# Down projections of the MLPs: a fourth step of seven products in each second half, and residual banks added by DMA

## The reference, cut to what matters

```python
h = rms_norm(x, norm_mlp_g[l])
x = x + jnp.square(jax.nn.relu(h @ w_mlp_up[l])) @ w_mlp_down[l]      # 2048 -> 8192 -> 2048
```

## Time and profile before

| | us |
|---|---|
| median of 3 timed runs | 2652.4 (2650.54 to 2652.66) |
| the profiled execution | 2650.98 |
| its span, first to last instruction | 2649.3 |
| TensorE matmul busy in it | 2640.2 |
| VectorE busy | 1986.9 |
| ScalarE busy | 1366.9 |

### The profile page before, as it was taken

How to read it: one execution, slowest core, us unless ns; L and a number is a source line. 1 busy time by engine, 2 the same in 40 slices (tenths; PEclk the granted TensorE clock), 3 DMA queues, 4 the chain that set the end, 5 groups by cost and what they waited for, 6 DMA issues and landing times.

```text
span 2649.3 us, 39598 instructions
## 1 busy us (share of the span) xinstructions
PE 2640.2 (100%) x13478; PEld 2233.5 (84%) x13478; DVE 1986.9 (75%) x2876; ACT 1366.9 (52%) x1865; POOL 30.3 (1%) x64
## 2 busy tenths in 40 slices
PE   9999999999999999999999999999999999999999
PEld 7888888888888888888888888888788888888887
DVE  6687876555555778798797567878787978879886
ACT  6455555444444554555554454456555555455453
POOL 0100000000000000000000000000000000000000
PEclk9999999999999999999999999999999999999999
DMA  7655556665655566556566555545555655655565
GB/s 277 236 175 182 190 173 197 204 201 194 203 191 188 177 199 205 187 196 198 190 206 210 190 176 175 173 150 191 171 175 190 199 198 192 205 190 196 187 205 175
DMA packets 141721, 511.06 MB, mean 193 GB/s; under 512 B 16134, under 2 KB 16439, under 8 KB 141464
## 3 DMA queue, kind: packets, MB, share of 16 engines
q1 hardware_dynamic: 136312, 493.86, 55.9%
q0 software_dynamic: 3840, 12.86, 1.5%
q10 hardware_dynamic: 1440, 2.62, 0.3%
HBM read 505.08 MB, written 4.21 MB: 192 GB/s over the span
## 4 chain that ended last, share of the span: by engine, by line
PE 96%; DVE 2%; ACT 1%; DMA 0%; issue 0%; SPq 0%; ACTq 0%; DVEq 0%
PE acc L1955 26%; PE acc L1952 13%; PE acc L1973 5%; PE acc L1991 4%; PE acc L1993 4%; PE acc L1992 4%; PE pS L1991 3%; PE pS L1993 3%; PE pT L1993 3%; PE pT L1991 3%; PE pS L1992 3%; PE pT L1992 3%; PE acc L1970 2%; PE pO L1991 2%; PE pO L1993 2%; PE pG L1993 2%
## 5 line engine op out<-in xcount | busy, mean ns | idle before, releaser
L1104 DVE TENSOR_TENSOR wlo<-raw,whi 128x1024 fp32r<-128x1024 f32 x938 | 1143.4, 1223 | 446.4 <-ACT whi L614 440.5
L614 ACT ACTIVATE whi<-raw 128x1024 fp32r<-128x1024 f32 x938 | 990.0, 1057 | 793.7 <-PE pT L1993 243.1
L1955 PE MATMUL acc<-a_w,whi 128*128 128x512 f32 x2944 | 935.8, 397 | 0.1
L1952 PEld LDWEIGHTS acc<-a_w,wlo 128*128 128x128 f32 x2944 | 553.2, 188 | 129.4
L1952 PE MATMUL acc<-a_w,wlo 128*128 128x256 f32 x2944 | 578.6, 278 | 0.0
L1955 PEld LDWEIGHTS acc<-a_w,whi 128*128 128x128 f32 x2944 | 451.5, 189 | 2.5 <-DVE a_w L1157 0.8
L1973 PE MATMUL acc<-a_w,whi 128*128 128x512 f32 x592 | 198.4, 404 | 0.0
L825 ACT ACTIVATE t<-acc 128x256 f32<-128x256 f32 x128 | 48.9, 382 | 170.0 <-PE acc L1955 169.9
L1970 PEld LDWEIGHTS acc<-a_w,wlo 128*128 128x128 f32 x592 | 111.4, 188 | 24.5
L1970 PE MATMUL acc<-a_w,wlo 128*128 128x256 f32 x592 | 116.8, 279 | 0.0
L1500 DVE TENSOR_TENSOR t<-acc,t 128x256 f32<-128x256 f32 x128 | 54.0, 422 | 74.9 <-ACT t L825 74.8
(11 more groups left out here) (496 smaller groups left out, 3962.8 us busy)
## 6 DMA issues: line engine op xcount, KB each, us to landing
raw<-stream SPq DMA_DIRECT2D x938, 512.0 KB, 3.4
gbias<-gateb POOLq DMA_DIRECT2D x12, 256.0 KB, 4.1
X<-x_rows POOLq DMA_DIRECT2D x4, 512.0 KB, 6.8
bias_scratch<-brow POOLq DMA_DIRECT2D x8, 256.0 KB, 5.5
q<-bias_scratch POOLq DMA_DIRECT2D x8, 256.0 KB, 3.8
out<-X ACTq DMA_DIRECT2D x8, 256.0 KB, 5.3
xF<-x SPq DMA_DIRECT2D x6, 256.0 KB, 6.8
bias<-bias_scratch POOLq DMA_DIRECT2D x8, 128.0 KB, 4.1
```

Of the source, the lines that this page charges most:

```text
L614: A(whi[:, slot, :], raw[:, slot, :], ACT.Copy).then_inc(s.hi_done, 1)
L1104: TT(wlo[:, slot, :], raw[:, slot, :], whi[:, slot, :].bitcast(F32), SUB).then_inc(s.lo_done, 1)
L1952: low = lambda: MM(ps[:, 0:T], wl, wide[:, k0 + k, 0:T], start=False, stop=False, skip_group_check=True)
L1955: last = MM(ps, wh, wide[:, k0 + k, :], start=start and k == 0, stop=not start and k == KC - 1, skip_group_check=True)
```

## The change

`BLOCK_STEPS` becomes 0 to 3 in both halves, and both halves have one order: 4, 0, 1, 5, 2, 6, 3, 7 (ordinary, seven, seven, ordinary, seven, ordinary, seven, ordinary). In the six groups with two such halves the result banks are no longer added to X by VectorE: ScalarE copies each, scaled, to one of six SBUF buffers (`drain_bank`), and a DMA issued by GpSimd adds the buffer to X (`accum_op`). The part banks of g = 0 are copied by ScalarE; those of g = 1, 2 are added by VectorE at t = 14 and 15 of either half. `WARM` is 8. The GpSimd DMAs' descriptor scratch is set to 4096 bytes.

```diff
-WARM = 5
+WARM = 8
-BLOCK_ORDER = ((4, 0, 5, 1, 6, 2, 7, 3), (3, 4, 0, 5, 1, 2, 6, 7))
-BLOCK_STEPS = ((0, 1, 2, 3), (0, 1, 2))
+NDRAIN = 6
+DRAINS = 8 * 3
+BLOCK_ORDER = ((4, 0, 1, 5, 2, 6, 3, 7), (4, 0, 1, 5, 2, 6, 3, 7))
+BLOCK_STEPS = ((0, 1, 2, 3), (0, 1, 2, 3))
...
+        drain = sb("drain", NDRAIN * COLS)[0].rearrange("p (k c) -> p k c", k=NDRAIN)
...  GpSimd
+            def add(dst):
+                k = added[0]
+                added[0] += 1
+                pool.dma_start(dst, drain[:, k % NDRAIN, :], accum_op=ALU.add).then_inc(drain_added[k % NDRAIN], 16)
+            def add_columns(i, n):
+                for h in range(2):
+                    pool.wait_ge(s.t_evac, 2 * (i + n) + h + 1)
+                    add(X[:, h, COLS * n:COLS * n + COLS])
...  ScalarE
+            def drain_bank(ps, scale, freed):
+                k = drained[0]
+                drained[0] += 1
+                if k >= NDRAIN:
+                    act.wait_ge(drain_added[k % NDRAIN], 16 * (k // NDRAIN))
+                A(drain[:, k % NDRAIN, :], ps, ACT.Copy, scale=scale).then_inc(freed, 1)
+            def drain_parts(layer, g, q):
+                r = phase(layer, g, q)
+                act.wait_ge(s.block_done, BLOCK_CHUNKS_AFTER[r])
...
+                for n in range(4):
+                    A(parts[q][n], (acc[0], acc[1], pV, pN)[n], ACT.Copy).then_inc(s.m_free, 1)
+                    def down_pair(q):
...
+                        for t in range(16):
+                            if t == 14 and not g:
+                                drain_parts(layer, g, q)
+                            if t == 14 and not q:
+                                act.wait_ge(s.rb_ready, 4 if layer else 2)
+                                act.wait_ge(s.t_evac, 2 * i)
+                            if t >= 14:
+                                act.wait_ge(s.t_half, i + t - 13)
+                                column(t - 14, 0)
+                                act.wait_ge(s.mm_done, c + t + 1)
+                                column(t - 14, 1)
+                            prep(At(c + t))
...  VectorE, down_pair
-                            if q and t in (1, 2):
-                                part_sums(layer, g, 0, (0, 1) if t == 1 else (2, 3))
-                            if q and t in (12, 13):
-                                part_sums(layer, g, 1, (0, 1) if t == 12 else (2, 3))
+                            if g and t >= 14 and (layer, g) in SECOND_GROUPS:
+                                part_sums(layer, g, q, (0, 1) if t == 14 else (2, 3))
...  VectorE, last group of a layer, after up unit 1
+                        if ends and m == 1:
+                            drains_landed(dve, layer)
+                            dve.wait_ge(s.t_evac, done)
...
-    nc = bacc.Bacc("TRN2", target_bir_lowering=False, num_devices=1)
+    nc = bacc.Bacc("TRN2", target_bir_lowering=False, num_devices=1, dynamic_dma_scratch_size=4096)
```

More of the change, by code:

```diff
@@ L478, in program @@
         wg_landed = [ctx.enter_context(nc.semaphore(f"wg_landed{k}")) for k in range(2)]
+        drain_added = [ctx.enter_context(nc.semaphore(f"drain_added{k}")) for k in range(NDRAIN)]
         gb_landed = [ctx.enter_context(nc.semaphore(f"gb_landed{k}")) for k in range(2)]
@@ L492, in phase, with drains_landed @@
             return BLOCK_PHASES.index((layer, g, q)) if (layer, g, q) in BLOCK_PHASES else None
+        def drains_landed(eng, layer):
+            for k in range(NDRAIN):
+                eng.wait_ge(drain_added[k], 16 * len(range(k, DRAINS * (layer + 1), NDRAIN)))
         def block_tile(p, m):
@@ L574, in _, with add_drains @@
                     pool.dma_start(gbias[n % 2], gateb[:, D * g + COLS * q:D * g + COLS * q + COLS]).then_inc(gb_landed[n % 2], 16)
+            added = [0]
+            def add(dst):
[6 more added lines that the diff above has]
+                    add(X[:, h, COLS * n:COLS * n + COLS])
+            def add_drains(layer, i0):
+                for g in range(FF_GROUPS - 1):
+                    i = i0 + 4 * g
+                    add_columns(i, 0)
+                    add_columns(i, 1)
+                    add_columns(i, 2)
+                    add_columns(i, 3)
+            add_drains(0, G_MLP1)
             pool.wait_ge(s.m_added, 8)
@@ L807, in _ @@
                             mix_hi(At(3))
+            drained = [0]
+            def drain_bank(ps, scale, freed):
[7 more added lines that the diff above has]
+                act.wait_ge(s.block_done, BLOCK_CHUNKS_AFTER[r])
+                if layer and not g:
+                    act.wait_ge(s.m_added, 8)
+                if r and not g:
+                    act.wait_ge(s.m_free, 4 * r)
+                for n in range(4):
+                    A(parts[q][n], (acc[0], acc[1], pV, pN)[n], ACT.Copy).then_inc(s.m_free, 1)
             def mlp(b, a, i0, layer, stage, gain, before):
@@ L860, in mlp @@
                         up(At(15))
-                    for n in range(NG):
-                        down(n, g == FF_GROUPS - 1)
+                    if (layer, g) in SECOND_GROUPS:
+                        down_pair(0)
+                        down_pair(1)
+                    else:
+                        for n in range(NG):
+                            down(n, g == FF_GROUPS - 1)
             mlp(B_MLP1, A_MLP1, G_MLP1, 0, 1, "g_mlp1", G_OUT1 + NG - 1)
@@ L1976, in half_unit, with chunk_tok @@
                 last.then_inc(s.mm_done, 1)
-            def chunk_tok(c, i, banks, src, k0, first, last, units=None, corner=False):
+            def chunk_tok(c, i, banks, src, k0, first, last, units=None):
                 slot = c.mod(NSLOT)
@@ L1992, in chunk_tok @@
                         MM(ps, hi, wl, start=False, stop=False)
-                        end = MM(ps, lo, wh, start=False, stop=(last or (corner and h == 1)) and k == 1)
+                        end = MM(ps, lo, wh, start=False, stop=last and k == 1)
                     if last and h == 0:
@@ L2008, in block_step, with product @@
                 c12 = tbanks(At(i + 1), True)[0]
-                def product(ps, left, right, fresh=False, last=last):
+                def product(ps, left, right, fresh=False, last=False):
                     MM(ps, left[0], right[0], start=fresh, stop=False)
@@ L2016, in block_step @@
                 pe.wait_ge(s.lo_done, c + 1)
-                end = product(c11, a(1, 0), w(0, 1))
-                if last:
-                    end.then_inc(s.t_half, 1)
+                product(c11, a(1, 0), w(0, 1))
                 if first:
```

46 lines of the change are left out of this document (12 added, 34 removed).

## The result

| | before | after |
|---|---|---|
| median of 22 runs each | 2650.76 us | 2655.01 us |
| lowest to highest | 2650.28 to 2652.66 | 2653.55 to 2656.21 |
| profiled execution | 2650.98 | 2655.06 |
| its span | 2649.3 | 2653.4 |

The ratio is 1.0015, with a 95% interval of 1.0009 to 1.002. The changed kernel is slower by about 4 us. That is within the 0.2% that I had called no change, but the interval leaves out a ratio of 1, so it is a real difference. In the terms of the sum, 2652.1 was forecast for the profiled execution and 2655.06 came: 3.0 us are missing. The median before is 2650.76 over 22 runs, where the forecast had only three, with a median of 2652.4.

What follows compares the result with a forecast made beforehand. TensorE (PE) was taken as the bound, its matmuls filling 2640.2 of 2649.3 us. 2650.98 - 4.1 - 1.9 + 6.9 + 0 + 0.2 = 2652.1, plus 0.2 for the median: 2652.3 us, range 2646 to 2660.

Steps and rivals of the forecast that it cites:

- Part 1: Down phases: six second halves get one more step of seven products, 18 matmuls fewer at 0.227 us, -4.1 us.
- Part 2: PE's wait for the part banks at a second half's first step of seven goes, six times 0.31: -1.9 us.
- Part 3: Before the up units after g = 1 and 2: PE waits 1.73 us for part sums, four times, +6.9 us.
- rival B: PE does not wait before the up units, the part sums being done in time: 2645.2 us, chance 0.10.
- Part 4: VectorE's load at adjacent steps of seven: 0; only a delay x above 0.5 us costs PE, x - 0.5.
- Part 5: 48 adding DMAs and drains replacing VectorE's additions: 0, stream loads 1 to 2 us late for two or three chunks.
- Rival C: Adds hold stream loads, or DVE, before an adjacent pair beyond its 0.5 us: 2662 or 2676 us, chance 0.17.
- Rival D: The sixth gain of Part 1 is lost elsewhere, for example in waits for corner banks: 2656 us, chance 0.05.
- Part 6: Start: six more warm-up records at the upper clock level end at 9.7 to 9.8, first chunk was 9.53: +0.2 us.

Runs made afterwards that it cites:

- experiment 5: Experiment 1's kernel with three instead of four steps of seven in the second half: 2650.2 us, ratio 0.9999.
- Experiment 9: The kernel before with the first half's four part sums all at t = 1 instead of two at t = 1 and two at t = 2: 2649.18 us.
- Experiment 1: The changed kernel with all four part sums of g = 1 and 2 at t = 14, ahead of the subtraction: 2646.49 us, ratio 0.9983.
- Experiment 6: Experiment 1's kernel with each stream load after the first four chunks cut to half its columns: 2644.6 us, ratio 0.9976.
- experiment 2: The changed kernel with the 48 adding DMAs cut to 64 bytes a row instead of 2 KB: 2653.91 us, ratio 1.0013.
- experiment 11: Experiment 1's kernel with the adds cut to 64 bytes a row: 2645.95 us, ratio 0.9981.
- Experiment 3: The kernel before with WARM = 8 instead of 5, nothing else changed: 2650.73 us, ratio 0.9999.
- 8: Experiment 1's kernel with the second half's order 4, 0, 5, 1, 6, 2, 3, 7: 2651.49 us, ratio 1.0003.
- 12: The kernel of experiment 8 with the adds cut to 64 bytes a row: 2644.79 us, ratio 0.9977.
- 7: Experiment 1's kernel with the 48 adding DMAs made plain copies of the same bytes: 2646.2 us, ratio 0.9983.

## Why the prediction was right and wrong

**Part 1** held: 18 matmuls fewer; experiment 5 gives 3.7 us for the steps as a whole. **Part 2** held in the trace, but not for the reason that opens it: from the last step of seven to the next need of the part banks it was two ordinary steps and 0.68 us before as well. The wait goes because the sums no longer stand between the subtractions behind the boundary. Experiment 9, which moves two of them one chunk earlier in the old order, measured 1.4 of the 1.9.

**Part 3** held in mechanism and place, in four places and not after g = 0. That forecast and reading are both 1.73 us is partly luck: the start that the part works out is 1.63 late, not 1.73, since ScalarE's drain moved its next instruction by 0.52 and not 0.61, and the 0.1 that the late matmul costs beyond that was not in the part. Experiment 1 removed the wait by order alone. So rival B, that the wait would not come, was wrong, though its kernel exists: it is experiment 1, at 2646.49, where B gave 2645.2.

**Part 4 is the step that failed:** "The step before each pair is ordinary, as it was, so the first has some 3.0 us in hand and the second 3.0 - 2.53 = 0.5." The part takes the cover of every pair from VectorE's and PE's instructions and does not ask when the loads land. In the first halves, behind the light up units, that held: in six of the seven the first step had 3.1 us in hand and the second 0.43 to 0.46 (2.74 and 0.17 in (0, 0)), and PE waited in none. In the second halves it did not. VectorE comes out of the first half's last step of seven behind PE, works that off in four back-to-back subtractions, and each releases a slot, so several loads start close together, and those of chunks 3 to 5 land after 4.3 to 5.6 us instead of 3.5. The second half's first step then had 1.5 to 2.8 us in hand and the second 0.05 to 0.24, and PE waited. The part's own rule, "PE loses x - 0.5", even gives the price: the first step of (0, 0) had 1.71 us in hand, so x is 3.09 - 1.71 = 1.38 and the loss 0.9, where 0.99 was read; the same in (1, 1) makes 1.06, where 1.14 was read. Only x was put at nothing without a reason. Experiment 6 shows that it was the loads: with them halved, 3.08 and 0.55 come back and no wait stays. PE waiting for `sums_lo` or `wlo` anywhere in a half was also named as a sign that the forecast is wrong, and it came.

**Part 5** failed in one sentence, "the chunks loaded then come behind the adjacent pair. I take **0**". The adds held the queues 2.2 times as long as plain copies and took a third to a half of the 3.2 us of lateness in after (experiment 2), though only about 0.5 us once the part sums stood together (experiment 11). The estimate of "1 to 2 us late for two or three chunks" was somewhat low (chunks 6 and 7 took 4.7 to 6.2 against 3.5, so 1.2 to 2.7 late); what I missed is that VectorE already ran on loads there, the pair's chunks 4 and 5 included, which were still under way when the adds began.

**Rival C** had the right place (a pair, beyond its 0.5 us) and the wrong price: +10 or +24 against 3.2 measured. Its second branch, POOL's issues holding VectorE, did not come: while POOL issued four adds from 1002.74 to 1006.3, VectorE's four sums took 0.68 and 0.69 us, and its subtraction at 1216.56, beside two other issues, took 1.23, as elsewhere. The rule of the Trainium skill that part 5 weighed (page SBUF — State Buffer, section Who interferes with whom) speaks of GpSimd instructions that read SBUF; this kernel shows no effect of it for an instruction of POOL that only issues a DMA. **Rival D** named the loss of part 1's gain elsewhere, 2656; in effect 3.2 of 4.1 us were lost so, but in waits for VectorE's weights, not for corner banks.

**Part 6** had the wrong limit for the start: the first chunk starts at 9.07 instead of 9.53, not 0.2 later. Timeline of after, VectorE and PE:

```profile
7.70 1.23 DVE L1181 TENSOR_TENSOR wlo<-raw,whi 128x1024 fp32r<-128x1024 f32 x1 [1.40 <-ACT whi L647]
...
9.07 0.47 PE L2049 MATMUL acc<-whi,a_w 128*128 128x512 f32 x1
```

The first chunk follows VectorE's first subtraction by 0.14 us here and by 0.15 before, where that subtraction began at 8.15: its input had landed sooner in this launch, and the six matmuls more just fitted in front of it. PE's matmuls of the warm-up also reached the upper level some 0.8 us sooner: their records are down from 0.85 to 0.49 us at 6.54, before at 7.28. Experiment 3 shows nothing for the median.

**The time.** 2652.3 against 2655.01: the sum missed the 3.2 us of the second halves' steps, and the start gave 0.65 back. The range held, and so did "within 0.2%". But against the median of 2652.4 that I had, the forecast was a gain of 0.1 us, and a loss of 4.2 came against the median of 22 runs. That the forecast lies only 2.7 off owes something to the three early runs, two of which were near 2652; from 2650.76 the same sum gives 2651.9.

## What to carry to other kernels

An engine in order is late by what is queued in front of the instruction that frees a bank, so look first at what that is: moving two sums ahead of one subtraction removed 6.95 us of waits (8.5 us of the time), more than the 4.1 of the matmuls saved. A cover read in the middle of a phase is not that of its start: follow the reserve of the feeding engine across the boundary, with the loads that its own catching up releases all at once. And the bytes of the same 48 transfers cost about 0.5 us or 6.7 us depending on which loads they meet (experiments 1 and 11, 8 and 12), so an order is to be judged together with its transfers.

## What the runs showed of the hardware

- A DMA that adds 256 KB within SBUF lands after 6.3 us in the median, a plain one in the same place after 4.4 (experiments 1 and 7); with loads of half the bytes beside them, adds land after 4.4 too (experiment 6). An add has 64 packets more (10752 against 7680 on the queue, with 48 of them) and holds the 16 engines 2.2 times as long. POOL issues it in 0.86 us, a plain one in 0.54.
- The median landing of the stream's loads rose only from 3.4 to 3.5 us, while those of the chunks 3 to 5 of a second half, which decided, took 4.3 to 5.6. A median over 938 loads says little of eighteen.
- With 5 warm-up matmuls, 13 of 103 executions had a granted clock of 0.999 over the launch; with 8, none of 136 (experiment 3).
